# A mixture-of-experts kernel whose per-tile row lists go through a small table in DRAM

## The reference, cut to what matters

```python
probs = softmax(t @ router_w)                       # 512 x 16
sel = probs + router_bias
g_idx = argmax(sum of the two largest of sel in each group of 4)
e_idx = the two best experts of that group
wts = probs[e_idx] / sum                            # two weights per token
g, u = t @ w_gate[e], t @ w_up[e]                   # 1024 -> 512, for the chosen experts
y = sum over the two experts of wts * ((silu(g) * u) @ w_down[e])
```

## Time and profile before

| | |
|---|---|
| median of 3 runs | 770.80 us (769.92 to 770.91) |
| the profiled execution: its own time, its span | 770.69 us, 768.8 us |
| PE busy, DVE busy, ACT busy, POOL busy | 743.4 (97%), 599.6 (78%), 392.2 (51%), 195.8 (25%) us |
| mean granted TensorE clock | 0.995 of full |
| `index` products on PE (line 1772) | 68 matmuls, 8.6 us busy |
| `select` on DVE (line 1298) | 68 instructions, 18.9 us busy |
| gathers, scatters on POOL | 18 of mean 2.016 us, 14 of mean 7.628 us |

### The profile page before, as it was taken

How to read it: one execution, slowest core, us unless ns; L and a number is a source line. 1 busy time by engine, 2 the same in 40 slices (tenths; PEclk the granted TensorE clock), 3 DMA queues, 4 the chain that set the end, 5 groups by cost and what they waited for, 6 DMA issues and landing times.

```text
span 768.8 us, 10951 instructions
## 1 busy us (share of the span) xinstructions
PE 743.4 (97%) x3500; PEld 612.6 (80%) x3501; DVE 599.6 (78%) x824; ACT 392.2 (51%) x360; POOL 195.8 (25%) x80
## 2 busy tenths in 40 slices
PE   7899999999999999999999899999999999999995
PEld 6788888776888888887788587888888888888884
DVE  4894426764674765758768899999999999999985
ACT  4546333324232231324345267777777777777744
POOL 1000004102000000000064111555555555555533
PEclk9999999999999999999999999999999999999999
DMA  8989414211375563917472818899999999999895
GB/s 299 318 271 389 151 55 147 72 56 57 109 267 170 167 215 123 313 55 273 170 265 85 318 44 294 308 370 393 365 366 364 363 358 384 373 369 374 313 187 168
DMA packets 108709, 187.18 MB, mean 243 GB/s; under 512 B 7096, under 2 KB 58360, under 8 KB 108685
## 3 DMA queue, kind: packets, MB, share of 16 engines
q1 hardware_dynamic: 101276, 173.58, 62.7%
q0 software_dynamic: 5792, 11.65, 5.6%
q10 hardware_dynamic: 1616, 1.65, 0.6%
HBM read 180.47 MB, written 15.73 MB: 255 GB/s over the span
## 4 chain that ended last, share of the span: by engine, by line
PE 85%; DVE 8%; DMA 3%; issue 1%; ACT 1%; SPq 1%; DVEq 0%; POOLq 0%; ACTq 0%
PE ps L1522 25%; PE ps L1523 25%; PE ps L1524 25%; DVE wsplit L843 3%; PE ps L1782 2%; DMA raw<-in_w_ada 2%; PE ps L1886 1%; PE ps L1652 1%; DVE raw L932 1%; PE ps L1713 1%; DMA raw<-in_w_out 1%; DMA work<-hf_rows,tok_idx 1%; PE ps L1818 1%; PE ps L1772 1%; DVE raw L886 1%
## 5 line engine op out<-in xcount | busy, mean ns | idle before, releaser
L843 DVE TENSOR_TENSOR wsplit<-raw,wsplit 128x2048 fp32r<-128x2048 f32 x128 | 289.8, 2289 | 57.0 <-ACT wsplit L565 34.2
L752 ACT ACTIVATE wsplit<-raw 128x2048 fp32r<-128x2048 f32 x96 | 183.8, 1921 | 69.4 <-PE ps L1524 69.4
L512 POOL DMA_INDIRECT expert_rows<-work,dest_now x14 | 106.8, 7628 | 105.2 <-DVE work L1402 97.3
L1522 PE MATMUL ps<-wsplit,hgT 128*128 128x512 f32 x264 | 104.5, 396 | 1.3 <-DVE hgT L1313 1.3
L1524 PE MATMUL ps<-wsplit,hgT 128*128 128x512 f32 x264 | 103.1, 390 | 0.0
L1523 PE MATMUL ps<-wsplit,hgT 128*128 128x512 f32 x264 | 102.9, 390 | 0.0
L1522 PE MATMUL ps<-hT,wsplit 128*128 128x512 f32 x256 | 101.1, 395 | 1.0 <-DVE mx L1028 1.0
L1524 PE MATMUL ps<-hT,wsplit 128*128 128x512 f32 x256 | 99.7, 390 | 0.0
L1523 PE MATMUL ps<-hT,wsplit 128*128 128x512 f32 x256 | 99.7, 390 | 0.0
L886 DVE SCALAR_TENSOR_TENSOR raw<-raw,c_silu 128x256 f32 (+1 forms) x128 | 62.0, 485 | 12.6 <-DMA raw<-in_w_ada 8.6
L520 POOL TENSOR_TENSOR wsplit<-raw,wsplit 128x2048 fp32r<-128x2048 f32 x2 | 9.2, 4614 | 198.3 <-ACT wsplit L565 198.2
(11 more groups left out here) (299 smaller groups left out, 1278.3 us busy)
## 6 DMA issues: line engine op xcount, KB each, us to landing
raw<-in_w_exp_gate SPq DMA_DIRECT2D x32, 1024.0 KB
raw<-in_w_exp_up SPq DMA_DIRECT2D x32, 1024.0 KB
raw<-in_w_exp_down SPq DMA_DIRECT2D x32, 1024.0 KB
raw<-in_w_in SPq DMA_DIRECT2D x20, 1024.0 KB
raw<-in_w_ada SPq DMA_DIRECT2D x16, 1024.0 KB
raw<-in_w_ada SPq DMA_DIRECT2D x16, 512.0 KB, 5.9
expert_rows<-tmp SPq DMA_DIRECT2D x4, 1024.0 KB, 11.4
raw<-in_w_branch_a SPq DMA_DIRECT2D x4, 1024.0 KB
```

The source lines that it names most:

```text
L512: g.indirect_dma_start(out=y_dram, out_offset=bass.IndirectOffsetOnAxis(ap=dest_now[:, 0:1], axis=0), in_=y, in_offset=None, bounds_check= ...
L752: A_(wsplit[:, c, 0, :], raw[:, c, :], ACT.Copy).then_inc(hi_ready, 1)
L843: V.tensor_tensor(wsplit[:, n, 1, :], raw[:, slot, :], wsplit[:, n, 0, :].bitcast(F32), ALU.subtract).then_inc(lo_ready, 1)
L1522: nc.tensor.matmul(out, w_hi, m_hi_, start=first, stop=False)
```

## The change

For tiles 0, 1 and 2 the lists of tokens still come from selection matrices and index products, now with the token alone. For all tiles together DVE works out, once, the slot of every pair (its tile and its row in the tile) in a table of 128 x 24 records of four words; POOL writes the 1024 records (token, result row, weight) into a DRAM table by eight indirect DMAs of 128 records (`place`), and reads the table back into SBUF by one DMA. From then on tile j's tokens, result rows and weights are three columns of that table. The copies of a list into the fixed place where an indirect DMA takes it from are now POOL's own (`tok_now`, `dest_now`), `select`, `index`, `indices` and `destination` are gone from the loop, and so is the gather behind the last tile.

```diff
@@ sync
                     if n == U0 + 1:
+                        sp.wait_ge(table_empty, 1)
+                        sp.dma_start(table_dram.rearrange("(p i) c -> p i c", p=P), table[:, :, :]).then_inc(table_reset, 16)
                         sp.wait_ge(zero_row, 1)
...
-            wait_reg(sp, gathered, tiles * 16 + 16)
+            wait_reg(sp, hg_t, tiles)
@@ gpsimd
+            g.memset(record[:, :, :, 3], 0.0)
+            g.memset(table[:, :, 2:4], 0.0)
+            g.memset(table_i[:, :, 0:2], SKIP).then_inc(table_empty, 1)
+            g.iota(record_i[:, :, :, 0], pattern=[[P, NT], [0, 2]], base=0, channel_multiplier=1)
+            g.iota(record_i[:, :, :, 1], pattern=[[2 * P, NT], [1, 2]], base=0, channel_multiplier=2)
...
+            def early_gather(j):
+
+                pool.wait_ge(idx_ready, j + 1)
+                if j:
+                    pool.wait_ge(hg_t, j)
+                gather_rows(tok_idx)
+
             def gather(j):
...
+                wait_reg(pool, gathered, j * 16)
+                g.tensor_copy(tok_now[:, :], table_wi[:, ds(j * 4, 1)]).then_inc(tok_ready, 1)
+                wait_reg(pool, tok_ready, j - 2)
+                wait_reg(pool, hg_t, j)
+                gather_rows(tok_now)
 
             def scatter(j):
 
+                if not isinstance(j, int):
+                    wait_reg(pool, scattered, j * 16)
+                g.tensor_copy(dest_now[:, :], table_wi[:, ds(j * 4 + 1, 1)]).then_inc(dest_ready, 1)
+                wait_reg(pool, dest_ready, j + 1)
                 wait_reg(pool, y_ready, j + 1)
...
+            def place(which):
+
+                for t in range(NT):
+                    g.indirect_dma_start(out=table_dram,
+                                         out_offset=bass.IndirectOffsetOnAxis(
+                                             ap=slot_of[:, which * NT + t:which * NT + t + 1], axis=0),
+                                         in_=record[:, t, which, :], in_offset=None, bounds_check=P * TILES_MAX - 1,
+                                         oob_is_err=False).then_inc(table_filled, 16)
...
-            for j in range(4):
-                gather(j)
+            early_gather(0)
+            pool.wait_ge(table_reset, 16)
+            pool.wait_ge(slots_ready, 1)
+            place(0)
+            early_gather(1)
+            place(1)
+            early_gather(2)
+            pool.wait_ge(table_filled, 16 * 2 * NT)
+            pool.dma_start(table[:, :, :], table_dram.rearrange("(p i) c -> p i c", p=P)).then_inc(table_in, 16)
+            pool.wait_ge(table_in, 16)
+            gather(3)
             pool.wait_ge(y_zero, 16 * NT)
             scatter(0)
...
-            gather(tiles)
-            wait_reg(pool, gathered, tiles * 16 + 16)
+            wait_reg(pool, gathered, tiles * 16)
@@ vector
+            step(V.scalar_tensor_tensor(out=r_over, in0=pos_all, scalar=float(2 * P), in1=r_over, op0=ALU.is_gt, op1=ALU.add))
...
+            step(V.tensor_tensor(part_of, chosen, r_slot.unsqueeze(1).broadcast_to(both), ALU.mult))
+            done()
+            step(V.tensor_reduce(r_slots.rearrange("p (c t) -> p c t", c=2),
+                                 part_of.rearrange("p c (t e) -> p c t e", e=E), AX_X, ALU.add))
+            done()
+            V.tensor_copy(slot_of[:, :], r_slots).then_inc(slots_ready, 1)
...
                 dve.wait_ge(chunk_used, used)
-                dve.wait_ge(idx_ready, j + 1)
+                dve.wait_ge(table_in, 16)
                 dve.wait_ge(scattered, j * 16)
...
-                    select(i + 2, e2)
                     lo_c(0)
...
-                if prev:
-                    indices(i + 2)
                 lo_c(3)
...
-                if prev:
-                    destination(i - 1)
                 a_lo(i)
@@ tensor
                 gate_up(i, i * 6 + 30, 0, between)
-                index(i + 2, e2)
                 turn(i + 1)
```

More of the change, by code:

```diff
@@ L245, in tokens_moe_kernel, with row_weight @@
         r_n, r_first, r_wrap, r_i = (small(TILES_MAX) for _ in range(4))
-        r_extra = small(1)
+        r_extra, r_wrapped = small(1), small(1)
+        r_base, r_far, r_slots = small(E), small(NT), small(2 * NT)
+        r_slot, r_over = r_sel, r_top
+        record_i = record[:, :, :, :].bitcast(I32)
+        table_i = table[:, :, :].bitcast(I32)
+        table_w = table[:, :, :].rearrange("p i c -> p (i c)")
+        table_wi = table_w.bitcast(I32)
+        def row_weight(j):
+            return table_w[:, ds(j * 4 + 2, 1)]
         sub_ready = sem("sub_ready")
@@ L1443, in _ @@
             done()
-            dve.wait_ge(idx_mm, tiles + 1)
+            dve.wait_ge(idx_mm, 3)
             for j in range(TAIL):
@@ L1462, in _ @@
             y_53 = ps[:, 5:7, :].rearrange("p b n -> p (b n)")
[L1463 removed]
+            V.scalar_tensor_tensor(out=y_53, in0=y_53, scalar=row_weight(tiles - 2), in1=gf, op0=ALU.mult,
                                    op1=ALU.mult).then_inc(y_ready, 1)
@@ L1765, in _, with index @@
             mm.then_inc(pos_mm, 1)
-            def index(j, e):
+            def index(j):
                 pe.wait_ge(sel_ready, j + 1)
@@ L1819, in turn_hidden @@
                 mm.then_inc(a_trans, 1)
-            def expert_ahead(i):
-                return pe.value_load(expert_of[0:1, ds(i + 2, 1)], min_val=0, max_val=E - 1)
             unread_products(4)
             pe.wait_ge(gf_ready, 2)
-            pe.wait_ge(sel_ready, 1)
-            for t in range(NT):
-                mm = nc.tensor.matmul(ps[:, 7, 0:2], sel[:, t, :], info[:, t, 0, 0:2], start=(t == 0), stop=(t == NT - 1))
-            mm.then_inc(first_mm, 1)
-            unread_products(4)
-            pe.wait_ge(weights_ready, 1)
-            for t in range(NT):
-                mm = nc.tensor.matmul(ps[:, 6, 0:2], sel[:, t, :], info[:, t, 0, 2:4], start=(t == 0), stop=(t == NT - 1))
-            mm.then_inc(idx_mm, 1)
-            unread_products(5)
-            index(1, 1)
+            index(0)
+            unread_products(10)
+            index(1)
             unread_products(6)
@@ L1859, in _, with tile @@
                 mm.then_inc(chunk_used, 1)
-            def tile(i, e2, between=None):
+            def tile(i, between=None):
                 gate_up(i, i * 6 + 30, 0, between)
-                index(i + 2, e2)
                 turn(i + 1)
@@ L1866, in tile @@
                 turn_hidden(i)
-            tile(1, expert_ahead(1), between=lambda: turn_hidden(0))
+            tile(1, between=lambda: turn_hidden(0))
+            pe.wait_ge(tiles_ready, 1)
             tiles = pe.value_load(expert_of[0:1, 31:32], min_val=0, max_val=7) + E
             with pe.Fori(2, tiles - 1) as i:
-                tile(i, expert_ahead(i))
+                tile(i)
             gate_up(tiles - 1, tiles * 6 + 24, 0)
@@ L1892, in _ @@
             pe.wait_ge(tail_lo, 2)
-            pe.wait_ge(idx_ready, tiles + 1)
+            pe.wait_ge(idx_ready, 3)
             for t in range(2):
```

97 lines of the change are left out of this document (50 added, 47 removed).

## The result

The changed kernel takes 763.1 us (median of 4, 762.28 to 764.08) beside 770.86 for the kernel before: ratio 0.9908, 95% interval 0.9895 to 0.9921. The profiled execution took 764.08, the longest of its four; its span is 762.2 against 768.8, so the traces have 6.6 us to explain.

What follows compares the result with a forecast made beforehand. PE, DVE and the DMA queues were all taken to be at their limit, with the loads deciding. The traced 770.69 less 4.2 for the loop plus 0.2 for tile 1's gather gave 766.7 us, range 764.5 to 772.3.

Steps and rivals of the forecast that it cites:

- Loop, both together: Tile loop up to tile 16: loads, not PE alone, set its first products at 722.4, a gain of 4.2 us.
- the head start: Loads' lead at the loop's start, from an expert's second tile reusing weights; claimed used up just as the loop ends.
- Loop, POOL: POOL's one-word copies before each DMA in the loop: gather and scatter wait as before, cost zero.
- the index group: Four index products on PE before each tile's turn: 0.36 us each tile, 14 removed save 5.0 us.
- Rival 1: Tile loop: loads give way and PE sets the pace, gain 5.9 us, time 764.8 us; chance 0.13.
- Rival 2: Loop: POOL's gather slips behind two more subtracts in every tile, taking the gain back, 770.7 us; chance 0.17.
- Start of the loop: DVE ahead of tile 2: less select and list work starts its products 0.85 us earlier, at 471.2.
- Prologue: Before the loop: DVE's subtract at 433.7 is covered; POOL's table writes delay tile 1's gather to 440.3, costing 0.2 us.
- Rivals 3 and 4: Prologue: subtracts hold tile 1's gather until 446.7 (772.3 us, chance 0.13), or behind the first only (769.1 us, chance 0.12).

Runs made afterwards that it cites:

- part 3: Two edits of the changed kernel: POOL's loop scatter made to wait for the next tile's hidden product, 763.31 us; select put back behind each tile's first subtract, 764.94 us.

## Why the prediction was right and wrong, by its steps

**What failed: "Loop, both together".** It let the load stream run on at the rate of the earlier trace rows, to land chunk 2 of tile 16 at 714.1 and start the products at 722.4. That load was there 4.1 us before its copy at 710.55, and the products began at 720.01. Reading the head start from the earlier trace rows was right: in the kernel before, the lead was 0.7 us at tile 16. For that kernel the rate was right too (18.3 by the estimate of part 3). Wrong was to take it for a property of the queues. The full share is not a limit, since one core's queues show 1.00 at 371 GB/s, 1.01 at 381 and 1.03 at 391. And the change itself raised the rate that the loads can reach: without the select, POOL's scatter is held by one subtract instead of three, and the lead holds. That the two go together is shown by the runs of part 3; why is open. In the prediction's terms two more places failed with it. "DVE loses 1.3 of its 18.1 us, so it can follow" counted DVE's time and not what stands behind it on POOL. And "Loop, POOL", put at zero because the scatter would be held till the end of a subtract run as before, overlooked that this end comes two subtracts earlier: 2.20 us instead of 7.66. With the select kept, loads did run short at the end, and the time was 765.5; that this is near the forecast is chance, since the forecast was for a kernel without it.

**Mis-sized: the index group.** 0.36 a tile was its own span; with the turn and the down products behind it, which it makes longer, it cost 0.455. Over 14 tiles that is 6.4 us, not 5.0.

**Rival 1** (loads give way, 764.8) had the mechanism; with the group at 0.455 and the front gain as it came, its sum gives 770.69 - 0.2 - 6.4 = 764.1, the profiled time.

**Rival 2** fell: the gather behind POOL's copy starts 16 us before the turn that wants its rows (608.74; the turn 17.71 behind 607.00), and PE never waits there in the loop.

**Start of the loop.** Forecast: 0.85 earlier, less 0.2 for the gather of tile 1. It came 0.2 earlier, with all ahead of it some 0.2 later in this execution (the first turn at 436.49, not 436.25); from the first turn to rows_lo of tile 2 it was 34.01 us (to 470.50) instead of 34.44 (to 470.69), so 0.43 of the 0.65. PE's wait at tile 1's turn (0.4, put at 0.2) was foreseen. Not foreseen was the clock. In both kernels PE waits for the first rows (3.07 us before, 3.46 after) and the granted clock is then at half for 3.4 us. Before, that began at 437.3, when the turn of 436.25 was nearly done; after, it began at 436.8, within the turn, which took 1.75 us instead of 1.09 (1.09 again, at clock 1.00, in the run with more unread products). The step from rows_lo to the next subtract run was 7.33 us (470.50 to 477.83), as worked out.

**Prologue.** The subtract forecast for 433.7 started at 433.94. A write that nothing holds takes POOL 0.98, near the 0.95 of the forecast, but 0.30 lies between two, so 1.29 apart: the gather began at 441.33 instead of 440.3, 0.8 us ahead of the subtract (442.15) that would have caught it. The Trainium skill (DMA: Bandwidth & Descriptors, "Anatomy of one DMA") gives a DMA issued from GpSimd a fixed cost of about 2.0 us; that POOL is bound for that long is not what this trace shows. **Rivals 3 and 4** didn't happen, but their mechanism is real: four writes more made PE wait 8.4 us, and the kernel was slower than before the change.

## What to carry to other kernels

A DMA share of 1.00 was no ceiling here; whether loads are late is read from who ended the wait of the engine that consumes them, here PE in every tile. Relief of an engine has to be followed to what that engine holds up: a 1 us instruction on DVE cost POOL 5.4 us, and with it went the head start of the loads. After this change PE's 17.71 us a tile stand 0.11 above the loads' 17.60, so a further relief of PE pays in full only while the head start lasts: 0.91 us less in each of 14 tiles, 12.7 us, bought 6.2 us (762.8 to 756.62).

## What the runs showed of the hardware

The same scatter takes 2.20, 4.36 (the first one after the change) or 7.66 us: it ends about 0.9 us behind the first, second or third of a run of subtracts with two SBUF inputs. The Trainium skill (SBUF — State Buffer, "Who interferes with whom") says that such an instruction contends with a POOL instruction that reads SBUF. The runs agree, but which of the ends lets POOL in is not explained by them: a scatter that starts 0.97 us into a run of subtracts comes through behind the first, one that starts 1.03 us into it behind the second, and those that start 0.43 us into it (the 7.17 us of the earlier trace rows) or up to 0.1 us ahead of it are held for all three. The DMA share of one core can read 1.03. Eight transposes take 0.87 us behind 512-column products and 0.95 behind four products of two or four columns; four take 0.44 and 0.52.
